# Reordering the projection, transpose and score products of a gated linear attention stage on TensorE

## What is computed

```python
h = rmsnorm(x, norm_mix_w)
gq, gk, gv, ggate, ga, dq, dk, dv, dgate = split_cols(h @ w_in)
g = log_sigmoid(ga @ w_alpha2 + b_alpha2) / 16
# per head and chunk of 64 tokens, G = cumsum(g):
q_dec, k_inv, k_end = q * exp(G), k * exp(-G), k * exp(G_last - G)
scores = where(causal, q_dec @ k_inv.T, 0)
kv     = k_end.T @ v                      # state = decay * state + kv
o      = scores @ v + q_dec @ state
o_gla  = head_rmsnorm(o, gla_norm_w) * silu(ggate)
# then: differential attention on dq, dk, dv, dgate; output projection; cross-attention; final norm
```

## Time and profile before

| What | Value |
|---|---|
| Median of 3 runs | 832.19 us (832.1 to 832.24) |
| Time of the profiled execution | 832.24 us |
| Its span in the trace | 830.5 us |
| Granted TensorE clock, mean | 0.998 of full speed |
| TensorE busy with products | 814.6 us, 98% |
| VectorE busy | 587.0 us, 71% |
| ScalarE busy | 437.8 us, 53% |
| The 16 GLA steps | about 79 to 204 us of the span |

### The profile page before, as it was taken

How to read it: one execution, slowest core, us unless ns; L and a number is a source line. 1 busy time by engine, 2 the same in 40 slices (tenths; PEclk the granted TensorE clock), 3 DMA queues, 4 the chain that set the end, 5 groups by cost and what they waited for, 6 DMA issues and landing times.

```text
span 830.5 us, 13216 instructions
## 1 busy us (share of the span) xinstructions
PE 814.6 (98%) x4586; PEld 683.7 (82%) x4586; DVE 587.0 (71%) x1360; ACT 437.8 (53%) x1057; POOL 83.6 (10%) x123
## 2 busy tenths in 40 slices
PE   7999999999999999999999999999999999999997
PEld 6887888888788888878888898888888888888885
DVE  6788668767578667767857877599845564367997
ACT  7865445445445445445545666543655464356543
POOL 3100122210000111111100000000010000001201
PEclk9999999999999999999999999999999999999999
DMA  9321359972144245655512168955331121206945
GB/s 295 107 82 39 108 169 190 183 135 73 33 134 112 77 80 98 124 96 121 109 61 83 59 192 244 280 156 141 126 103 60 56 64 39 90 13 134 215 96 202
DMA packets 70410, 99.21 MB, mean 119 GB/s; under 512 B 6597, under 2 KB 38473, under 8 KB 70345
## 3 DMA queue, kind: packets, MB, share of 16 engines
q1 hardware_dynamic: 52360, 64.29, 24.4%
q0 software_dynamic: 15392, 29.36, 19.6%
q10 hardware_dynamic: 2592, 4.72, 1.8%
HBM read 83.68 MB, written 31.46 MB: 139 GB/s over the span
## 4 chain that ended last, share of the span: by engine, by line
PE 92%; DVE 5%; ACT 1%; issue 1%; DMA 0%; POOL 0%; ACTq 0%; DVEq 0%
PE bank L1842 14%; PE bank L1844 14%; PE bank L1843 14%; PE banks2to L1842 10%; PE banks2to L1844 10%; PE banks2to L1843 10%; PE banks6to L1914 4%; PE banks2to L2101 3%; PE bank L2124 2%; DVE neg_max L1641 2%; PE banks2to L2037 1%; PE bank L2126 1%; PE banks6to L2061 1%; DVE w_lo L1380 1%; PE banks6to L1844 1%
## 5 line engine op out<-in xcount | busy, mean ns | idle before, releaser
L1844 PE MATMUL bank<-w_hi,actT_lo 128*128 128x512 f32 x412 | 161.3, 391 | 0.0
L1842 PE MATMUL bank<-w_hi,actT_hi 128*128 128x512 f32 x384 | 154.8, 403 | 0.3
L1843 PE MATMUL bank<-w_lo,actT_hi 128*128 128x512 f32 x384 | 149.6, 390 | 0.0
L1380 DVE SCALAR_TENSOR_TENSOR w_lo<-w_raw,vecs,w_hi 128x512 fp32r<-128x512 f32 x120 | 86.8, 750 | 43.3 <-ACT w_hi L1098 43.3
L1844 PEld LDWEIGHTS bank<-w_hi,actT_lo 128*128 128x128 f32 x412 | 77.3, 188 | 16.9
L1098 ACT ACTIVATE w_hi<-w_raw,vecs 128x512 fp32r<-128x512 f32 x120 | 82.5, 719 | 8.3 <-DMA w_raw<-in_w_ckv 4.2
L1842 PEld LDWEIGHTS bank<-w_hi,actT_hi 128*128 128x128 f32 x384 | 73.0, 190 | 15.1 <-DVE w_lo L1380 1.5
L1843 PEld LDWEIGHTS bank<-w_lo,actT_hi 128*128 128x128 f32 x384 | 72.3, 188 | 13.4
L984 POOL TENSOR_TENSOR rs_o<-var_o,neg_half 128x1 f32<-128x1 f32 (+1 forms) x48 | 28.9, 602 | 379.3 <-DVE var_o L1668 256.9
L1844 PE MATMUL banks2to<-w_hi,actT_lo 128*128 128x512 f32 x164 | 64.0, 390 | 0.0
L1263 ACT ACTIVATE prob<-banks2to,neg_maxs 128x128 f32<-128x128 f32 (+7 forms) x64 | 47.0, 741 | 15.2 <-DVE neg_maxs L1642 15.0
(11 more groups left out here) (368 smaller groups left out, 2045.1 us busy)
## 6 DMA issues: line engine op xcount, KB each, us to landing
w_raw<-in_w_in SPq DMA_DIRECT2D x56, 256.0 KB, 3.2
out_sums<-in_w_out POOLq DMA_DIRECT2D x11, 1024.0 KB, 9.7
late_sums<-in_w_co POOLq DMA_DIRECT2D x11, 1024.0 KB, 9.2
w_raw<-in_w_ckv SPq DMA_DIRECT2D x32, 256.0 KB, 3.5
w_raw<-in_w_cq SPq DMA_DIRECT2D x32, 256.0 KB, 2.8
stage_in<-in_x SPq DMA_DIRECT2D x8, 512.0 KB, 4.6
tile_a<-mixed ACTq DMA_DIRECT2D x16, 256.0 KB, 3.3
x_res<-in_x SPq DMA_DIRECT2D x8, 512.0 KB, 6.1
```

The source lines that it names most:

```text
L1380: return dve.scalar_tensor_tensor(dst, src, scale, hi.bitcast(F32), ALU.mult, ALU.subtract)
L1842: pe.matmul(dst, l_hi, r_hi, start=start, stop=False)
L1843: pe.matmul(dst, l_hi, r_lo, start=False, stop=False)
L1844: return pe.matmul(dst, l_lo, r_hi, start=False, stop=stop)
```

## The change

Three things change in the GLA steps, and no instruction is added or left out. Projections alternate between bank0 and bank1. A projection s (1 to 15) is cut in three: its k step 0 (`proja`) stands behind the rest of projection s-1 and ahead of output s-2 and scores s-1; k steps 1 and 2 (`projb`) stand behind key-value s-1; k steps 3 to 7 follow the transpose. The transpose of the keys goes to bank 2, where head 0's scores are, from step 1 on: it waits for the masked copy (`sc_cp`) of the step before, and the scores wait for the split of the transposed keys.

```diff
+OPENED = 3
@@
-    plan.extend([("rope",), ("proj", 0), ("gmul", 0)])
+    plan.extend([("rope",), ("proj", 0), ("gmul", 0), ("proja", 1)])
     for s in range(GLA_STEPS):
         plan.append(("scp", s))
         if s:
             plan.append(("ovar", s - 1))
         plan.extend([("sc", s), ("kv", s)])
         if s + 1 < GLA_STEPS:
-            plan.extend([("qk", s + 1), ("kdT", s + 1)])
+            plan.extend([("qk", s + 1), ("projb", s + 1), ("kdT", s + 1)])
         passed = [("ofin", s - 1)] if s else []
         if s + 1 < GLA_STEPS:
-            plan.extend([*passed, ("proj", s + 1), ("gmul", s + 1), ("o", s)])
+            plan.extend([*passed, ("proj", s + 1), ("gmul", s + 1)])
+            plan.extend([("proja", s + 2)] if s + 2 < GLA_STEPS else [])
+            plan.append(("o", s))
@@
         def proj_bank(s):
+            if s < GLA_STEPS:
+                return banks[s % 2]
             return banks[5] if s in SIDE_BANK else bank0[:, :]
+
+        def kd_bank(s):
+            return banks[2 if s else 1]
@@ ScalarE and VectorE read proj_bank(s) for bank0 and kd_bank(s) for bank1
@@ TensorE, kdT
                     wait(pe, kd_dve, s)
-                    pe.transpose(bank1[:, 0:P], k_end[:, p, cols(t)], ident[:, :]).then_inc(kd_pe, 1)
+                    wait(pe, sc_cp, s)
+                    pe.transpose(kd_bank(s)[:, 0:P], k_end[:, p, cols(t)], ident[:, :]).then_inc(kd_pe, 1)
@@ TensorE, proj: starts at k step 3 where the projection was opened
+                    first = OPENED if s < GLA_STEPS else KT // 2
@@ TensorE, new
+                elif kind in ("proja", "projb") and w[0] < GLA_STEPS:
+                    s = w[0]
+                    if s == 1 and kind == "proja":
+                        pe.wait_ge(kd_dve, 1)
+                    if kind == "proja":
+                        wait(pe, pj_dve, s - 1)
+                    project(("proj", s), proj_bank(s), activations(cols(s % TT)),
+                            lambda k, slot: (w_hi[:, slot, :], w_lo[:, slot, :]),
+                            0 if kind == "proja" else 1, 1 if kind == "proja" else OPENED)
@@ TensorE, sc
                     wait(pe, sc_cp, s)
                     if s == 0:
                         pe.wait_ge(z_act, 2)
+                    else:
+                        pe.wait_ge(kd_dve, s + 1)
```

More of the change, by code:

```diff
@@ L1162, in _ @@
                         act.wait_ge(kv_pe, at("kv", s - 2))
-                    copy(ke_hi[:, s % 2, :], bank1[:, 0:P]).then_inc(kd_act, 1)
+                    copy(ke_hi[:, s % 2, :], kd_bank(s)[:, 0:P]).then_inc(kd_act, 1)
                 elif kind == "proj" and w[0] < GLA_STEPS:
@@ L1168, in _ @@
                         act.wait_ge(o_pe, at("o", s - 2))
-                    copy(v2[:, s % 2, 0, :], bank0[:, 0:256])
+                    copy(v2[:, s % 2, 0, :], proj_bank(s)[:, 0:256])
                     if s:
                         act.wait_ge(pj_dve, s)
-                    act.activation(tanh_g[:, :], bank0[:, 256:512], ACT.Tanh, scale=0.5).then_inc(pj_act, 1)
+                    act.activation(tanh_g[:, :], proj_bank(s)[:, 256:512], ACT.Tanh, scale=0.5).then_inc(pj_act, 1)
                 elif kind == "sc":
@@ L1522, in _ @@
                     dve.wait_ge(kd_act, s + 1)
-                    lo_part(ke_lo[:, s % 2, :], bank1[:, 0:P], ke_hi[:, s % 2, :]).then_inc(kd_dve, 1)
+                    lo_part(ke_lo[:, s % 2, :], kd_bank(s)[:, 0:P], ke_hi[:, s % 2, :]).then_inc(kd_dve, 1)
                 elif kind == "proj" and w[0] < GLA_STEPS:
@@ L1526, in _ @@
                     dve.wait_ge(pj_act, s + 1)
-                    lo_part(v2[:, s % 2, 1, :], bank0[:, 0:256], v2[:, s % 2, 0, :]).then_inc(v_dve, 1)
+                    lo_part(v2[:, s % 2, 1, :], proj_bank(s)[:, 0:256], v2[:, s % 2, 0, :]).then_inc(v_dve, 1)
                 elif kind == "gmul":
@@ L1532, in _ @@
                     dve.scalar_tensor_tensor(gate[:, 256 * (s % 2):256 * (s % 2) + 256], tanh_g[:, :], 1.0,
-                                             bank0[:, 256:512], ALU.add, ALU.mult).then_inc(pj_dve, 1)
+                                             proj_bank(s)[:, 256:512], ALU.add, ALU.mult).then_inc(pj_dve, 1)
                 elif kind == "scp":
@@ L1998, in _ @@
                         pe.wait_ge(tr_dve, at("tr", TT + 1, 1))
+                    first = OPENED if s < GLA_STEPS else KT // 2
                     last = project(stage, proj_bank(s), activations(cols(s % TT)),
                                    lambda k, slot: (w_hi[:, slot, :], w_lo[:, slot, :]),
-                                   KT // 2 if ("proja", s) in NTH else 0)
+                                   first if ("proja", s) in NTH else 0)
                     signal(last, stage, pj_pe)
+                elif kind in ("proja", "projb") and w[0] < GLA_STEPS:
[7 more added lines that the diff above has]
+                            0 if kind == "proja" else 1, 1 if kind == "proja" else OPENED)
                 elif kind == "proja":
```

## The result

The changed kernel takes 842.85 us (median of 4 runs, 842.79 to 842.97) against 832.14 us before on the same chip: slower by a factor of 1.0129, 95% interval 1.0116 to 1.0141. Forecast were 843.5 us in a range of 841.7 to 845.5.

The account below looks back on a forecast made before the run. TensorE, busy for 98% of the span, was taken as the bound. +12.2 us over 14 transpose intervals, +1.45 ahead and -2.35 behind made +11.3 on 832.24 us: 843.5 us, range 841.7 to 845.5.

Parts of the forecast that it names:

- the added wait decides: At the transpose of the keys: TensorE arrives 2.1 us behind the outputs, the masked copy releases it at 3.5; stall 1.4.
- the circle: Transpose to transpose with a weight: 0.17 + 4.12, outputs 1.18, take-up 0.05, VectorE 3.37, release 0.10, together 8.99 us.
- Weight steps: GLA steps with a single weight to split: 8.99 us from transpose to transpose instead of 7.87, in ten intervals.
- The three-weight step: Step 7, where three weights stand ahead of the output sum on VectorE: one interval of 8.34 us.
- Steps without a weight: GLA steps with no weight to split: 0.08 us won and lost again, three intervals staying at 7.63 us.
- Ahead of the first transpose: Step 0: key-value start unchanged, first transpose later by k steps 1 and 2 and 0.08 us: +1.45 us.
- Behind the last: After step 15's transpose: nine products fewer (-2.06 us) and the 0.34 us wait shrunk to about 0.05: -2.35 us.
- The price of taking the transpose away from the narrow products: Transpose between wide products on TensorE: 0.08 us more a step, from 0.05 to 0.11.
- The distance without a wait: On TensorE, from the end of the values' low half to the key-value products' start when nothing waits: 0.11 us.
- The lower end of the range: Whole kernel: 841.7 us, from bounds on take-up (-0.5), release (0.5), transposes (-0.8) and knock-on (0.5 either way).
- the circle of 7.87 us stays: Rival, 4%: the transpose's wait does not bind, VectorE and ScalarE still set weight steps at 7.87 us; 831.1 us.
- The clock rival: Rival, 2%: stalls of 1.4 us halve TensorE's clock once in each of four weight-step runs, 5.5 us each; 865.5 us.

Follow-up runs that it names:

- changed kernel with moved weights: Changed kernel with single weights split behind the masked copy of the scores instead of ahead of it: 829.06 us, ratio 0.9963.
- the old order with the same edit: Kernel before the change with single weights split behind the masked copy of the scores instead of ahead of it: 829.76 us, ratio 0.9970.
- OPENED = 5: Changed kernel with four k steps (1 to 4) instead of two between key-value products and transpose: 830.64 us, ratio 0.9982.
- OPENED = 2: Changed kernel with one k step less ahead of the transpose: 856.83 us, ratio 1.0294.
- the banks alone: Changed kernel's banks with the order of before, no k step opened early: 888.67 us, ratio 1.0662.
- OPENED = 1: Changed kernel with no k step between key-value products and transpose, only k step 0 opened early: 870.0 us, ratio 1.0451.

## Why the prediction was right

The step that carried it was "the added wait decides": TensorE comes to the transpose 2.1 us behind the outputs, the copy is there at 3.5. The trace has 2.17 (164.81 to 166.98) and 3.56, a stall of 1.39 us where 1.4 was forecast, and the terms of the circle one by one: outputs taken up after 0.05 us (taken 0.05), output sum to copy 3.37 (3.37), release 0.14 (0.10), transpose to outputs 159.37 to 163.64 = 4.27 (4.29), outputs 163.64 to 164.81 = 1.17 (1.18). Together 9.00 against 8.99.

- Weight steps: 8.99 forecast, 8.95 to 9.00 in eight. Missed were the first tiles of the two halves: their outputs have no product with a state for the first chunk, and they took 8.75 and 8.73 us. That is 0.5 us of the 0.65 by which 843.5 was over 842.85.
- The three-weight step: 8.34 forecast, 8.36 measured. Steps without a weight: 7.63 and 7.62.
- Ahead of the first transpose +1.45 forecast, 82.38 - 81.04 = +1.34 measured (the first transpose of before behind step 0 was at 81.04). Behind the last: -2.35 forecast; the next projection begins 5.52 us later (208.45) instead of 7.85, -2.33.
- The price of taking the transpose away from the narrow products, 0.08 us more a step out of a range of 0.05 to 0.11, was at the low end. In the changed kernel with moved weights a product starts at 166.09, then come the transpose and a product, and the next starts at 166.66. That is 0.57 us for two products (0.46) and the transpose, so the transpose costs 0.11; the first product behind the narrow ones costs 0.11 more than another (164.82 to 165.16). Together 0.22, against 0.17 in the old order: 0.05 more. Its steps still take 7.57 us against 7.61 in the old order with the same edit, since the key-value products start 0.11 us behind the scores and not 0.18. In weight steps the part behind the narrow products lies ahead of the stall and changes nothing.
- The distance without a wait, 0.11 us, was right: it stands at 164.88 to 164.99.
- The lower end of the range does not follow from its own terms: -0.5, -0.5, -0.8 and -0.5 us make 2.3, so 841.2 and not 841.7. The measured 842.85 lies within both.
- Of the rivals, "the circle of 7.87 us stays" comes near what OPENED = 5 shows (831.1 forecast, 830.64 measured), though there the wait at the transpose still binds by 0.24 us. The clock rival got 2% and did not come, but it was nearer than I had argued. I had weighed it against one idle of 0.84 us, while the stalls to come were of 1.4 us; with 1.92 us the clock fell behind the very first one. That it held at 1.23 us no row before the run could tell, so the 2% were too sure. Its price was too high for each fall: not all 24 products of a step slowed (5.5 us) but 7 or 8 with OPENED = 2, some 1.6 us.

Two expectations missed. That of the banks alone was worked out at full clock, as the clock had held in the changed kernel, and it took the output sum to follow the outputs, where the gate was later. That of OPENED = 1 left out the waits of the steps without a weight; its rival named the clock and came true.

## What to carry to other kernels

When a tile moves into another's bank, ask who frees that bank and what stands ahead of that instruction in its engine's queue: here the copy that frees it took 0.49 us and ended 3.37 us behind the start of the output sum, because a weight's split and a round trip to ScalarE were ahead of it; with the weight behind it that was 1.09 us. A wait on an engine that in turn waits for the waiting engine makes a circle, and its sum, not the busy time, is the step. Before reordering the engine that waits, look whether the late one can be reordered: one changed condition there gained 2.4 us, where two banks and opened projections had lost 10.7, and with it these cost nothing more.

## What the runs showed of the hardware

In these steps single stalls of TensorE between 1.3 and 3.0 us were followed by a lower clock, though not each of them. With 1.23 us of idle before ten transposes the granted clock stayed 1.00. With OPENED = 2 (ten of 1.92 us, one of 1.28) it fell behind the first already, but only behind 4 of 11 in all, and cost 6.4 us; with 2.8 us (OPENED = 1) behind 4 of 11; with 3.0 us behind all 11, down to a mean of 0.68 in one stretch, and the products slowed by it make up 21 us. The Trainium skill, "TensorE: Matmul & The Clock Gate", Part 1, has the rule that an idle array is clocked at half rate, 1.2 GHz; the runs agree in kind, with products 0.43 us apart at the lower level and 0.229 at the upper. The times vary more where it falls: 888.67 us comes with a spread of 5 us, 842.85 with one of 0.2.
